# Row sums of the second layer's output projection on GpSimd instead of VectorE

## What is computed

```
sgo = (sgo * jax.nn.silu(zs)) @ w_sg_out[l]
ga, gs = jnp.split(jax.nn.sigmoid(gm + b_merge[l]), N_BRANCHES, axis=-1)
y = ga * a + gs * sgo
x = x + y @ w_o[l]
...
return rmsnorm_2(x, final_g)
```

## Time and profile before

| what | value |
|---|---|
| median of 3 runs | 1262.26 (1262.21 to 1262.78) |
| the profiled execution | 1262.92, of which the span of the profile is 1261.2 |
| TensorE (PE) busy | 1241.1, 98% |
| VectorE (DVE) busy | 818.7, 65% |
| ScalarE (ACT) busy | 558.7, 44% |
| GpSimd (POOL) busy | 147.0, 12% |
| chain that ended last, by engine | PE 86%, DVE 7%, ACT 3%, issue 2%, POOL 1% |

### The profile page before, as it was taken

One profiled execution on the slowest core, in us unless ns is written; L12 is line 12 of the kernel. 1 busy time (PEld: TensorE's weight loads), 2 busy tenths in 40 slices (PEclk: granted clock), 3 DMA queues, 4 the chain that ended last, 5 costly groups with the idle time before them and its releaser, 6 DMA issues.

```text
span 1261.2 us, 15542 instructions
## 1 busy us (share of the span) xinstructions
PE 1241.1 (98%) x6018; PEld 1039.8 (82%) x6018; DVE 818.7 (65%) x1272; ACT 558.7 (44%) x966; POOL 147.0 (12%) x208
## 2 busy tenths in 40 slices
PE   9999999999999999999999999999999999999997
PEld 8878888888878888888888888878888888888885
DVE  6885667754687555665665579858875436436687
ACT  5456564652455333333332263437763343223344
POOL 0001341231000100100000000005550000000200
PEclk9999999999999999999999999999999999999999
DMA  6242323129564943793332233321105322332971
GB/s 201 67 108 65 84 76 93 51 84 231 186 167 146 254 135 100 224 210 100 100 129 89 91 97 108 122 68 38 63 3 189 111 82 86 102 99 88 234 171 76
DMA packets 119077, 149.03 MB, mean 118 GB/s; under 512 B 14358, under 2 KB 90204, under 8 KB 119004
## 3 DMA queue, kind: packets, MB, share of 16 engines
q1 hardware_dynamic: 105436, 115.53, 28.8%
q0 software_dynamic: 13552, 32.51, 11.9%
q10 hardware_dynamic: 16, 0.00, 0.0%
HBM read 142.78 MB, written 2.10 MB: 115 GB/s over the span
## 4 chain that ended last, share of the span: by engine, by line
PE 86%; DVE 7%; ACT 3%; issue 2%; POOL 1%; DVEq 0%; ACTq 0%; POOLq 0%
PE ps_mm L2454 57%; PE ps_mm L2489 9%; PE ps_s L2757 3%; PE ps_mm L2757 3%; PE ps_t L2757 2%; PE ps_o L2757 2%; DVE w_lo L1513 1%; PE ps_s L2615 1%; ACT w_hi L908 1%; PE ps_o L2646 1%; PE ps_o L2902 1%; PE ps_mm L2529 1%; PE ps_s L2668 1%; PE ps_t L2626 1%; PE ps_o L2695 1%
## 5 line engine op out<-in xcount | busy, mean ns | idle before, releaser
L2454 PE MATMUL ps_mm<-act_hi,w_hi 128*128 128x512 f32 x944 | 372.2, 394 | 1.1 <-DVE w_lo L1513 1.1
L2454 PE MATMUL ps_mm<-act_hi,w_lo 128*128 128x512 f32 x944 | 370.0, 392 | 0.0
L2454 PE MATMUL ps_mm<-act_lo,w_hi 128*128 128x512 f32 x944 | 369.8, 392 | 0.0
L1513 DVE TENSOR_TENSOR w_lo<-stage,w_hi 128x2048 fp32r<-128x2048 f32 (+5 forms) x98 | 205.2, 2094 | 127.8 <-ACT w_hi L908 127.6
L908 ACT ACTIVATE w_hi<-stage 128x2048 fp32r<-128x2048 f32 (+5 forms) x99 | 171.9, 1736 | 143.1 <-PE ps_mm L2454 65.6
L2454 PEld LDWEIGHTS ps_mm<-act_hi,w_hi 128*128 128x128 f32 x944 | 177.4, 188 | 37.2 <-DVE w_lo L1513 2.4
L2454 PEld LDWEIGHTS ps_mm<-act_hi,w_lo 128*128 128x128 f32 x944 | 177.3, 188 | 35.6
L2454 PEld LDWEIGHTS ps_mm<-act_lo,w_hi 128*128 128x128 f32 x944 | 177.4, 188 | 34.7
L2489 PE MATMUL ps_mm<-w_hi,act_hi 128*128 128x512 f32 (+2 forms) x144 | 52.7, 366 | 0.6 <-DVE lat L1643 0.5
L2489 PE MATMUL ps_mm<-w_lo,act_hi 128*128 128x512 f32 (+2 forms) x144 | 52.2, 362 | 0.0
L2489 PE MATMUL ps_mm<-w_hi,act_lo 128*128 128x512 f32 (+2 forms) x144 | 52.2, 362 | 0.0
(11 more groups left out here) (518 smaller groups left out, 2363.4 us busy)
## 6 DMA issues: line engine op xcount, KB each, us to landing
stage<-in_w_in SPq DMA_DIRECT2D x43, 1024.0 KB, 5.3
sums<-in_w_ffn_down POOLq DMA_DIRECT2D x16, 1024.0 KB, 9.4
stage<-in_w_ffn_gate SPq DMA_DIRECT2D x11, 1024.0 KB, 7.6
stage<-in_w_ffn_up SPq DMA_DIRECT2D x11, 1024.0 KB, 7.0
stage<-in_w_ffn_down SPq DMA_DIRECT2D x8, 1024.0 KB, 5.0
osum<-in_w_out POOLq DMA_DIRECT2D x6, 1024.0 KB, 9.3
tsum<-in_w_o POOLq DMA_DIRECT2D x6, 1024.0 KB, 8.4
stage<-in_w_out SPq DMA_DIRECT2D x4, 1024.0 KB, 4.9
```

Source lines behind the costliest of these rows:

```text
L1513: V.tensor_tensor(w_lo[:, s, 0:k * w], raw, w_hi[:, s, 0:k * w].bitcast(F32), ALU.subtract).then_inc(w_lo_made, 1)
L2454: ins = T.matmul(ps_mm[:, 2 * bank_slot + m, :], wt[:, kk, m * P:(m + 1) * P], acts[ap][:, kk, :], start=(r == 0), stop=(r == per - 1), sk ...
```

## The change

`row_sums` goes from VectorE's program to GpSimd's, with the same four instructions, each now waiting for the one before. In GpSimd's program the four row sums stand between the accumulating loads. Two waits are new: the first row sum waits until the mixing stage has left `tmp`, and the first load into `t1_y` waits until VectorE has made the residuals of the first four chunks, which read `gu` too. In the changed file lines behind L862 are shifted.

```diff
@@ GpSimd @@
+            def row_sums(i):
+
+                even, odd, a, b = gu[:, 2 * i, :], gu[:, 2 * i + 1, :], slice(0, 2 * P), slice(2 * P, S)
+                pool.wait_ge(y_sum, 2 * i + 2)
+                if i:
+                    pool.wait_ge(op_made, SUMMED_AT["wo"] + i)
+                else:
+                    pool.wait_ge(chunk_lo_made, SG_AT + KD)
+                linked_after(G.tensor_tensor(tmp[:, 1, a], even[:, a], even[:, b], ALU.subtract))
+                linked_after(G.tensor_tensor(tmp[:, 0, a], even[:, b], odd[:, b], ALU.subtract))
+                linked_after(G.tensor_tensor(tmp[:, 0, b], tmp[:, 0, a], even[:, a], ALU.subtract))
+                G.tensor_tensor(tmp[:, 1, b], odd[:, a], tmp[:, 0, b], ALU.add).then_inc(s_summed, 1)
...
             for i in range(2):
                 block_into(tsum[:, i, :], sum_landed, n, 1, 1, add=True)
+            row_sums(0)
             pool.wait_ge(sum_landed, 16 * (loads + 4))
             block_into(tsum[:, 0, :], sum_landed, n, 0, 0, add=True)
+            row_sums(1)
             pool.wait_ge(s_summed, SUMMED_AT["wo"] - 4 + 2)
+            pool.wait_ge(chunk_lo_made, Y_AT + 4)
             block_into(t1_y[:, :], t1_landed, n, 0, 0)
+            row_sums(2)
             pool.wait_ge(t1_landed, 32)
             block_into(t1_y[:, :], t1_landed, n, 0, 1, add=True)
+            row_sums(3)
             pool.wait_ge(w_lo_made, unit_of(n, "P6") + 1)
@@ VectorE @@
-            def row_sums(i):
-
-                even, odd, a, b = gu[:, 2 * i, :], gu[:, 2 * i + 1, :], slice(0, 2 * P), slice(2 * P, S)
-                dve.wait_ge(y_sum, 2 * i + 2)
-                if i:
-                    dve.wait_ge(op_made, SUMMED_AT["wo"] + i)
-                link(V.tensor_tensor(tmp[:, 1, a], even[:, a], even[:, b], ALU.subtract))
-                after(link(V.tensor_tensor(tmp[:, 0, a], even[:, b], odd[:, b], ALU.subtract)))
-                after(link(V.tensor_tensor(tmp[:, 0, b], tmp[:, 0, a], even[:, a], ALU.subtract)))
-                V.tensor_tensor(tmp[:, 1, b], odd[:, a], tmp[:, 0, b], ALU.add).then_inc(s_summed, 1)
...
                     if c < KD - 1:
                         chunk_lo(c)
-                row_sums(i)
             lo(U0["wo"] + 1)
```

## The result

The changed kernel takes **1269.93 us** (median of 4 runs, 1269.75 to 1270.29); the kernel before, measured beside it, takes 1262.31 (4 runs, 1262.21 to 1262.78). The ratio is 1.0058, with a 95% interval of 1.0045 to 1.0071: slower by 7.6 us, where 6.8 was forecast. The profiled execution took 1270.29, its span is 1268.6; before, 1262.92 and 1261.2.

The account below looks back on a forecast made before the run. TensorE was taken to set the pace. The last copy 7.24 late, plus 7.25 to P2, gives 6.70 later; with 0.13 for the restart +6.8 us, so 1269.1; range 1264.9 to 1272.1.

Parts of the forecast that it names:

- The price of one instruction: GpSimd's sum of two 128x256 tensors in the row sums: 0.74 us, between 0.645 and 0.926.
- the 0.926 of the one-tensor form: Upper price per GpSimd row-sum instruction, from a 128x256 form with one tensor; as a rival +9.8, 1272.1 us, chance 0.12.
- The blocking: VectorE and GpSimd in the changed stage: whoever starts first holds the other up until about 0.13 us before its end.
- The loop: Each unit, from second addition to second addition on VectorE: 11.99 us instead of 10.88, 1.11 behind per unit, three times.
- The last copy: ScalarE's copy of the fourth row sum in the last unit: starts at 1224.40, 7.24 us later than at 1217.16.
- The slack of 0.54: At the joint before P2: a fourth row sum later by more than 0.54 us delays the end.
- the step from the copy to P2: From ScalarE's copy of the fourth row sum to TensorE's possible start of P2, through VectorE's weight residual: 7.25 us.
- GpSimd's queue: Five GpSimd loads queued with the row sums, and the new wait for the chunk residuals, cost nothing.
- The clock: TensorE idles some 3.7 us in P6; the granted clock was expected not to fall there.
- The rival: Clock falls for P6's last 15 matmuls and P2's 24: up to 7 us on top (1276), chance 0.05.

Follow-up runs that it names:

- The two halves: Against the kernel before: three row sums on GpSimd with the fourth on VectorE, 1266.31 us; only the fourth on GpSimd, 1266.23 us.
- the filled kernel: The changed kernel with 14 extra matmuls in the wait before P6's last quarter: 1269.36 us, ratio 1.0054; run again, 1269.70 us, 1.0053.

## Why the prediction came out right, point by point

- **The price of one instruction**, taken as 0.74: 0.72 to 0.74 undisturbed. Interpolating between two sizes of the same operation was right; the 0.926 of the one-tensor form is another operation's price. The Trainium skill, "GPSIMD Engine Reference", section "Performance versus the Vector engine", has 1.96 times VectorE, measured on rows of 2048. At the 256 of this case it is 0.74 / 0.42 = 1.76, and the measurement decides: at 0.82 the sum would have come out 1.3 higher, at +8.1.
- **The blocking**, taken from two places far from the change: borne out in every unit. Predicted were 0.74, a held one near 1.1, 0.74 and 2.7; measured 0.74, 1.09, 0.74 and 2.67. The Trainium skill, "SBUF — State Buffer", section "Who interferes with whom", says that a VectorE instruction with two SBUF inputs contends with a GpSimd instruction that reads SBUF, under an exclusive lock, and that one with at most one SBUF input, outside the modes that use both ports, does not. The runs agree on both sides of that condition: 2.67 with two, 0.73 with one input from PSUM.
- **The loop**, 11.99: measured 11.95, and 11.94 with the last row sum on VectorE. **The last copy**, 7.24 late: 1223.74 - 1217.16 is 6.58, and with the 0.47 that this execution was ahead, 7.05. The two halves, measured apart at +3.16 and +3.50, add up.
- **The slack of 0.54 and the step from the copy to P2**: the copy to the end of P2's residual is 7.17 (1223.74 to 1230.91), against 7.19 before (1217.16 to 1224.35). P2 waits for that residual where the clock lets it, in the filled kernel 1.14 of the 1.2 foretold.
- **GpSimd's queue**, at nothing: no wait for a load appears among TensorE's, which are the ones in P1 (1.42; 1.7 foretold), in P6 (3.37; 3.7 foretold) and one of 0.44 near the end, for VectorE's weights, that stands in the trace of before as well.
- **The clock** is the step that failed: "So I expect no fall." It fell in both profiled executions of the change. I had read it off a stretch behind the last matmul, where it held for four microseconds, and one such stretch is no bound on another. In the trace of before the fall comes in the very next row:

```profile
1257.00:1259.00 2.00, 0.00 (x0) 0.00 (x0) 0.42 (x1) 0.00 (x0) 0.00 (x0) 0.74 0.70 275
```

and in the changed kernel it comes sooner behind the last matmul, within the four microseconds on which I had relied:

```profile
1262.00:1264.00 2.00, 0.00 (x0) 0.00 (x0) 1.63 (x8) 1.71 (x5) 0.00 (x0) 0.64 0.91 363
```

The changed kernel's last matmul starts at 1260.05, and between 1262 and 1264 the clock is at 0.64 on the mean, so for most of that stretch at its lower level. The rival had a chance of 0.05 and up to 7 us; by what was measured it should have had a large chance and a small price, since P6's slowed matmuls run mostly in the time in which P2's weights are not ready anyway. That cover is 1.2 us wide, so only a long fall shows: 1.3 in one execution, next to nothing in the other. The prediction had not counted that cover for this rival, so that its miss cost the forecast so little is luck.

So the forecast of +6.8 answers to the +6.6 of the row sums: some 5.5 of blocking, and the 1.1 that is left without it. The rest of the measured 7.2 to 7.6 is put down to the clock at times and to the scatter in the first 16 us; the medians can't divide these two.

## What to carry to other kernels

An instruction moved from VectorE to GpSimd is not priced by its own duration but by what VectorE does beside it: each GpSimd instruction here that met a long VectorE instruction with two SBUF inputs waited it out, and the chain of four was caught at its fourth link, its first or its second, by where the long one fell (2.67, 2.70 and 2.66). Count the whole loop, not the instructions moved: 1.6 us taken off an engine that was waiting anyway bought nothing, and made that engine the bound. If such work has to sit on GpSimd, let the long instruction beside it read one input from PSUM (1.2 us instead of 7.6 here, with other data in place of w_hi; what it would cost to have w_hi there was not measured), or make it wait for the short ones (3.5). Neither beats leaving the sums on VectorE.

## What the runs showed of the hardware that was not expected

How long TensorE idles does not by itself decide whether its clock falls. With the residual behind the row sum TensorE idled 2.6 before P6 and the granted clock stayed at 1.00. With only the last row sum on GpSimd it idled 1.96, and the clock fell after it had begun to work again; busy time by stretch, in that kernel:

```profile
1222.00:1223.00 1.00, 0.00 (x0) 0.00 (x0) 0.95 (x1) 0.98 (x2) 0.15 (x1) 1.00 0.25 18
1223.00:1224.00 1.00, 0.67 (x3) 0.53 (x4) 0.28 (x1) 0.99 (x4) 0.00 (x0) 0.91 0.79 123
1224.00:1224.50 0.50, 0.50 (x3) 0.40 (x2) 0.00 (x0) 0.50 (x2) 0.00 (x0) 0.50 1.12 201
```

The idle time ended at 1223.33; in the first row, all idle, the clock is at its full level, and it is at the lower one in the third, in which TensorE is busy throughout. And in the same kernel, the change, the clock fell at 1225.0 in one execution, 1.1 before TensorE went on, and in the other only as it went on: there the granted clock is 1.00 up to 1226.50, and P6 goes on at 1226.78. It stayed at the lower level for some thirteen matmuls of P6 in the first and nine in the second.
